# The second MLP's up projection as seven block products per pair of column tiles

## The chip, the cores and the metric

The kernel runs on one core of one Trainium2 chip. A core has five engines that run their own queues and meet at semaphores: TensorE (PE in the profile, its weight loads PEld), VectorE (DVE), ScalarE (ACT), GpSimd (POOL) and SyncE (SP), which here issues the loads. The metric is the device time of one execution in microseconds (us), lower is better. The median of three runs stands for a kernel.

## What is computed

Two transformer blocks for 1024 tokens of width 1024, all in fp32. The change lies in the last part of the second block:

```
h2 = rmsnorm(x, mlp_norm_g)
x = x + square(relu(h2 @ w_ff1)) @ w_ff2      # w_ff1 1024x4096, w_ff2 4096x1024
return rmsnorm(x, final_norm_g)
```

The kernel doesn't divide by the root mean square before the MLP. Since relu and square are homogeneous it carries x times the gains through both products, and takes the mean square of each token in as a factor on the residual (MS2) and in the last norm.

## The kernel before

Activations lie transposed: features on the 128 partitions, 1024 tokens along the free dimension, 8 chunks of 1024 columns for the width. PSUM has 8 banks of 512 fp32 columns. Every fp32 operand of a product is written as a high part (rounded to the matmul's type, fp32r) and a low part (the rest), and a product is three matmuls: high by high, high by low, low by high. A matmul takes a 128x128 tile of weights and 512 tokens.

The second MLP works through the 4096 hidden features in 8 groups of 512 (`mlp_products`, `mlp_act`, `mlp_dve`, `mlp_loads`, `mlp_splits`). A group has 8 weight tiles. Four are up tiles: 128 hidden columns, 8 chunks of contraction, 3 products and 2 token halves, which is 48 matmuls (L1213) into two banks. Four are down tiles: 256 output columns, 4 chunks of contraction, again 48 matmuls (L1223), into four banks. Banks 0 to 3 and 4 to 7 take turns. For each weight tile SP loads 512 KB into one of two RAW buffers, GpSimd writes the high part WHI (L782) and the low part WLO (L784), and TensorE waits for `s_w`. After an up tile ScalarE takes the relu from PSUM (L1731) and squares it into F2H (L1733), VectorE squares it in fp32 (L2405) and subtracts (L2408, F2L). After a down tile VectorE adds four banks to the sum F2SUM (L2421). The first additions are preceded by the residual times MS2 (L2416).

Ahead of the MLP stand 8 output products of the attention (`product`, L930), 48 matmuls each. After each of them VectorE adds it to X (L2660), ScalarE squares and makes the high part A2H, VectorE the low part A2L (L2664) and the sum of squares. Within the first group TensorE also makes the sums of squares per token (`root_sums`) and spreads their roots over the partitions (`root_spread`). The last group's down products (`last_down`, L1502) go in 8 pieces of 24 matmuls by token halves, with the transposes of finished token blocks (`final_t`) among them; ScalarE (`final_root`) and VectorE (`final_out`, L2691) close each block, and SP stores it.

The first MLP has, at its head and tail, blocks of half the tokens: 24 matmuls into one bank (`half_up`, L1160). Their relu and square go by halves of 512 tokens: ScalarE L1716 and L1718, VectorE `hidden_squared` (L2287, one input from PSUM) and `hidden_low` (L2295, both inputs from SBUF), and ScalarE makes the weights' high part, GpSimd the low part.

## Time and profile before

| what | value |
| --- | --- |
| median of three runs | 2884.7 us (2882.3, 2884.7, 2892.6) |
| span of the profiled execution | 2887.8 us |
| time of the profiled execution beside its span | the page gives the span alone |
| TensorE busy | 2805.4 us, 97% of the span, 14772 matmuls |
| mean granted TensorE clock | 0.991 of 2.4 GHz |
| VectorE, ScalarE, GpSimd busy | 51%, 26%, 36% |

Times in rows count from the start of the span. "x192" is a number of instructions. In the chain of work that ended last each row is a start, a length in us and the work that filled it; "issue" is time in which nothing shown was waited for. PEclk is the granted clock of TensorE, 1.00 at full speed.

### The profile page before, as it was taken

What the parts mean: (1) busy time and instruction counts of PE and PEld (TensorE: products, weight loads), DVE (VectorE), ACT (ScalarE), POOL (GpSimd) and SP (SyncE); (2) the same over time, 40 slices, a digit from 0 to 9 for tenths busy, and PEclk for the clock granted to TensorE, in tenths of its full rate; (3) what the DMA queues carried; (4) which work ended last, traced back from release to release, by engine and by line L of the source; (5) the groups of instructions that cost most, each with busy time, mean ns of one, the idle gap of its engine ahead of it and who ended that gap; (6) DMA issues with size and microseconds to landing.
All of it is one profiled execution on the core that took longest, in us unless ns stands there. A gap on an engine that the chain in (4) does not pass through costs nothing.

```text
span 2887.8 us, 36086 instructions
## 1 busy us (share of the span) xinstructions
PE 2805.4 (97%) x14772; PEld 2249.2 (78%) x14772; DVE 1467.7 (51%) x1829; ACT 741.4 (26%) x1092; POOL 1039.1 (36%) x462
## 2 busy tenths in 40 slices
PE   7999999999999999999999999899999999999998
PEld 4888887778888887776888466577888888888887
DVE  4853244643333334556999534996555423333324
ACT  5001124432011013454121456753111100011101
POOL 1433324444444444442132032101344444444434
PEclk9999999999999999999999999999999999999999
DMA  8531114222111122253132100002411111111112
GB/s 309 187 112 37 37 43 140 88 88 87 52 51 44 51 66 88 88 161 69 44 106 95 37 1 2 2 2 100 149 51 44 45 51 51 44 50 51 44 58 102
DMA packets 256236, 211.34 MB, mean 73 GB/s; under 512 B 23131, under 2 KB 240746, under 8 KB 255722
## 3 DMA queue, kind: packets, MB, share of 16 engines
q1 hardware_dynamic: 253082, 201.12, 22.7%
q10 hardware_dynamic: 3024, 8.39, 0.8%
q8 instruction: 93, 1.52, 0.2%
q14 instruction: 37, 0.30, 0.0%
HBM read 187.46 MB, written 20.97 MB: 72 GB/s over the span
## 4 chain that ended last, share of the span: by engine, by line
PE 80%; DVE 14%; ACT 3%; issue 2%; POOL 1%; DMA 0%; SPq 0%; ACTq 0%; DVEq 0%; POOLq 0%
PE PS L1213 18%; PE PS L1223 17%; PE PS L930 13%; PE PS L1160 9%; DVE MB L2490 6%; PE PS L1176 5%; PE PS L1460 3%; PE PS L914 3%; PE PS L1367 2%; PE PS L1425 2%; PE PS L1502 1%; DVE STEP L2592 1%; PE PS L1398 1%; DVE NMX L2624 1%; PE PS L1278 1%
## 5 line engine op out<-in xcount | busy, mean ns | idle before, releaser
L782 POOL TENSOR_TENSOR WHI<-RAW,ZERO 128x1024 fp32r<-128x1024 f32 x148 | 283.5, 1916 | 1079.1 <-PE PS L1213 284.9
L795 POOL TENSOR_TENSOR WLO<-RAW,WHI 128x1024 fp32r<-128x1024 f32 x112 | 269.8, 2410 | 475.4 <-ACT WHI L1617 475.4
L784 POOL TENSOR_TENSOR WLO<-RAW,WHI 128x1024 fp32r<-128x1024 f32 x148 | 407.0, 2750 | 11.6
L930 PE MATMUL PS<-H,WHI 128*128 128x512 f32 x864 | 271.0, 395 | 2.5 <-DVE L L2639 0.9
L1731 ACT ACTIVATE RL<-PS 128x1024 f32<-128x1024 f32 x48 | 49.3, 1027 | 870.8 <-PE PS L1213 870.8
L930 PE MATMUL PS<-L,WHI 128*128 128x512 f32 x864 | 267.4, 391 | 0.0
L930 PE MATMUL PS<-H,WLO 128*128 128x512 f32 x864 | 267.0, 390 | 0.0
L2405 DVE TENSOR_TENSOR FT<-RL 128x1024 f32<-128x1024 f32 x48 | 92.8, 1934 | 316.9 <-ACT RL L1731 316.9
L1617 ACT ACTIVATE WHI<-RAW 128x1024 fp32r<-128x1024 f32 x112 | 118.7, 1060 | 468.8 <-PE PS L1160 188.3
L1160 PE MATMUL PS<-H,WHI 128*128 128x512 f32 x496 | 197.5, 398 | 5.0 <-POOL WLO L795 4.4
L1160 PE MATMUL PS<-L,WHI 128*128 128x512 f32 x496 | 194.7, 392 | 0.0
L1160 PE MATMUL PS<-H,WLO 128*128 128x512 f32 x496 | 194.7, 392 | 0.0
L930 PEld LDWEIGHTS PS<-L,WHI 128*128 128x128 f32 x864 | 162.8, 188 | 34.6
L930 PEld LDWEIGHTS PS<-H,WHI 128*128 128x128 f32 x864 | 160.4, 189 | 37.7 <-issue 2.4
L930 PEld LDWEIGHTS PS<-H,WLO 128*128 128x128 f32 x864 | 162.7, 188 | 34.5
L2490 DVE TENSOR_SCALAR_CACHE_REDUCE MB<-SCO,CAND 128x384 bf16<-128x384 f32 (+2 forms) x198 | 174.3, 943 | 1.2
L2421 DVE TENSOR_TENSOR F2SUM<-F2SUM,PS 128x2048 f32<-128x2048 f32 x28 | 64.1, 2288 | 200.2 <-PE PS L1223 200.2
L1213 PE MATMUL PS<-A2H,WHI 128*128 128x512 f32 x512 | 157.8, 389 | 1.4 <-issue 1.4
L1213 PE MATMUL PS<-A2H,WLO 128*128 128x512 f32 x512 | 157.6, 389 | 0.0
L1213 PE MATMUL PS<-A2L,WHI 128*128 128x512 f32 x512 | 157.6, 389 | 0.0
L2624 DVE TENSOR_REDUCE NMX<-PS 128x1 f32<-128x128 f32 (+26 forms) x128 | 92.7, 724 | 124.5 <-PE PS L1370 110.1
L1223 PE MATMUL PS<-F2H,WHI 128*128 128x512 f32 x448 | 138.0, 389 | 1.3 <-ACT MS L1958 1.3
(384 smaller groups left out, 5498.9 us busy)
## 6 DMA issues: line engine op xcount, KB each, us to landing
RAW<-w_fc SPq DMA_DIRECT2D x96, 512.0 KB, 3.9
RAW<-w_ff SPq DMA_DIRECT2D x68, 512.0 KB, 3.6
RAW<-w_in SPq DMA_DIRECT2D x62, 512.0 KB, 4.0
ADA<-w_ada SPq DMA_DIRECT2D x32, 512.0 KB, 5.1
RAW<-w_out SPq DMA_DIRECT2D x24, 512.0 KB, 4.0
ADA_FIRST<-w_ada SPq DMA_DIRECT2D x16, 512.0 KB, 10.2
X<-x_scratch SPq DMA_DIRECT2D x2, 4096.0 KB, 13.6
GB<-gate_scratch SPq DMA_DIRECT2D x8, 1024.0 KB, 5.5
```

Of the source, the lines that this page charges most:

```text
L782: nc.gpsimd.tensor_add(WHI[j][:, 0:n], RAW[j][:, 0:n], ZERO[:, 0:1].to_broadcast([P, n])).then_inc(s_whi, 1)
L784: nc.gpsimd.tensor_sub(WLO[j][:, 0:n], RAW[j][:, 0:n], WHI[j][:, 0:n].bitcast(F32)).then_inc(s_w, 1)
L795: nc.gpsimd.tensor_sub(WLO[w % 2][:, :], RAW[w % 2][:, :], WHI[w % 2][:, :].bitcast(F32)).then_inc(s_w, 1)
L930: last = mm(bank(b + t), wt[:, k, :], half(a, (k + at) % KC, t), start=(k == 0 and n == 0), stop=(k == KC - 1 and n == 2))
L1160: last = mm(bank(w_bank(w)), wt[:, k, :], half(a, k, e), start=(k == 0 and n == 0), stop=(k == KC - 1 and n == 2))
L1176: last = mm(bank(w_bank(w) + c), wt[:, k, c * P:(c + 1) * P], half(a, k, e), start=(k == 0 and n == 0), stop=(k == 3 and n == 2))
L1213: last = mm(bank(b + t), wt[:, k, :], a[:, k * S + t * HALF:k * S + (t + 1) * HALF], start=(k == 0 and n == 0), stop=(k == KC - 1 and n == 2))
L1223: last = mm(bank(b + 2 * c + t), wt[:, k, c * P:(c + 1) * P], a[:, k * S + t * HALF:k * S + (t + 1) * HALF], start=(k == 0 and n == 0), st ...
L1617: A(WHI[w % 2][:, :], RAW[w % 2][:, :], ACT.Copy).then_inc(s_whi, 1)
L2405: V.tensor_tensor(FT[:, :], RL[i % 2][:, :], RL[i % 2][:, :], ALU.mult).then_inc(s_h32, 1)
L2490: V.tensor_scalar(mask(b), scores(b), CAND[:, b - 2:b - 1].bitcast(F32), 0.0, op, ALU.add, accum_out=REACH[:, b - 2:b - 1]).then_inc(s_dve, 1)
L2624: V.reduce_max(NMX[:, n % 2:n % 2 + 1], bank(2 * (n % 2), 2)[:, 0:w], AX, negate=True).then_inc(s_nm, 1)
```

## The change

The up projection of the second MLP is done by Strassen's identity in Winograd's form. The 4096 hidden columns are taken in 16 pairs of 128-column tiles (`PAIR_GROUPS2`). For a pair the product is a 2x2 block product: hidden tile (2), contraction half (2, four chunks each), token half (2, 512 tokens). Instead of eight block products it makes seven, `pair_unit(g, j)`, each of 12 matmuls (4 chunks, 3 products, 512 tokens) into one bank.

- The seven token-side operands (blocks AH and AL 0 to 6, each 4 pieces of 512) are sums and differences of the four quarters of the scaled x. VectorE and ScalarE make them while the output products run; block 5 and block 6 are made in the first pair.
- The weight-side operands: four of the seven are sums, made in place by VectorE (`weight_sum`, 128x512, four for each pair). ScalarE writes the high part of each (`unit_high`), GpSimd the low part (`unit_low`), through a ring of four buffers of 512 (QHI, QLO). A high part waits until the unit four before it has been multiplied.
- The results are combined by quadrants (hidden tile, token half). ScalarE copies the first product (P1C), VectorE adds it to the second and fifth (`second_read`, `third_read`), adds those to three quadrants (`quadrant_added`); for each of four quadrants ScalarE takes relu and square (high part), VectorE the fp32 square in PSUM (`quadrant_squared`) and the low part (`quadrant_low`).
- The down projection has the same number of matmuls, but now per pair: 4 tiles (256 output columns, 2 chunks) of 24 matmuls into four banks (`pair_down`), so VectorE's additions of four banks to the sum are 14 times 4 in place of 7 times 4. The first down tile of a pair takes the quadrants in turn, 6 matmuls each, and waits for each one's low part. F2SUM is now X itself.
- Loads: two of 512 KB for the two up tiles of a pair, when the seventh low part of the pair before is done, and four of 256 KB through two buffers DRAW; the third waits for the low part of the pair's first down tile.
- The last two pairs have their up products back to back, then come the 8 last down pieces, each as two units of 12 matmuls. ScalarE makes the high parts of all sixteen before `final_root`.
- All of it is written out instead of looped.

The core of the diff (regions, the loads, the loops of each engine; what prepares blocks 0 to 6, the final additions and `load_last` are left out):

```diff
-        A2H = region("A2H", K0, 8 * S, F32R)
-        A2L = region("A2L", Y0, 8 * S, F32R)
-        F2H = region("F2H", L0, 4 * S, F32R)
-        F2L = region("F2L", L0 + 4096, 4 * S, F32R)
-        F2SUM = region("F2SUM", H0, 8 * S)
-        MS2 = region("MS2", K0 + 12288, S)
-        GAIN = region("GAIN", X0, S)
-        OT = [region(f"OT{j}", K0 + 1024 * j, S) for j in range(4)]
+        BLOCK_AT = [K0, K0 + 8192, K0 + 4096, K0 + 12288, K0 + 16384, L0, L0 + 4096]
+        AH = [region(f"AH{j}", a, 4 * HALF, F32R) for j, a in enumerate(BLOCK_AT)]
+        AL = [region(f"AL{j}", a + 2048, 4 * HALF, F32R) for j, a in enumerate(BLOCK_AT)]
+        ACC2 = region("ACC2", K0 + 20480, S)
+        MS2 = region("MS2", K0 + 20480, S)
+        QRAW = [region(f"QRAW{j}", 1024 * j, S) for j in range(2)]
+        QHI = [region(f"QHI{j}", 2048 + HALF * j, HALF, F32R) for j in range(4)]
+        QLO = [region(f"QLO{j}", 4096 + HALF * j, HALF, F32R) for j in range(4)]
+        F2H = [region(f"F2H{j}", a, 2 * S, F32R) for j, a in enumerate([H0, K0])]
+        F2L = [region(f"F2L{j}", a + 2048, 2 * S, F32R) for j, a in enumerate([H0, K0])]
+        P1C, U2, U3 = [region(n, H0 + 4096 + HALF * j, HALF) for j, n in enumerate(["P1C", "U2", "U3"])]
+        RLQ = [region(f"RLQ{j}", H0 + 5632 + HALF * j, HALF) for j in range(2)]
+        DRAW = [region(f"DRAW{j}", H0 + 6656 + HALF * j, HALF) for j in range(2)]
+        F2SUM = X
...
+        UNIT_SOURCE = ((0, 0), (0, 0), (1, 0), (0, 1), (1, 0), (1, 1), (0, 1))
+        SUMMED = {2: 1, 1: 2, 4: 3, 6: 4}
+        QUADRANTS = [(0, 0), (1, 1), (1, 0), (0, 1)]
+        QUADRANT_BANK = [0, 1, 3, 2]
...
+            def load_up(g):
+                for j in range(2):
+                    if g:
+                        sp.wait_ge(s_w, MLP2 + unit(g - 1, 6) + 1)
+                    else:
+                        sp.wait_ge(s_w, MLP2 - 1 + j)
+                    sp.dma_start(k_n(QRAW[j], KC, P), w_tile(w_ff1_2, 0, KC, 256 * g + P * j, P)).then_inc(s_raw[j], 16)
+            def load_down(g, c):
+                n = 4 * g + c
+                if n >= 2:
+                    sp.wait_ge(s_w, MLP2 + unit((n - 2) // 4, 7 + (n - 2) % 4) + 1)
+                else:
+                    sp.wait_ge(s_mm, MLP2)
+                sp.dma_start(k_n(DRAW[c % 2], 2, 256), w_tile(w_ff2_2, 256 * g, 2, 256 * c, 256)).then_inc(q_draw[c % 2], 16)
...
+            load_up(0)
+            load_down(0, 0)
+            load_down(0, 1)
+            for g in range(PAIR_GROUPS2 - 2):
+                load_up(g + 1)
+                load_down(g, 2)
+                load_down(g, 3)
+                if g + 1 < PAIR_GROUPS2 - 2:
+                    load_down(g + 1, 0)
+                    load_down(g + 1, 1)
+            load_last(0)
+            load_last(1)
+            load_up(PAIR_GROUPS2 - 1)
+            for i in range(2, 6):
+                load_last(i)
...
+            def unit_low(n, src):
+                pool.wait_ge(s_whi, MLP2 + n + 1)
+                nc.gpsimd.tensor_sub(QLO[n % 4][:, :], src, QHI[n % 4][:, :].bitcast(F32)).then_inc(s_w, 1)
...
+                for j in range(7):
+                    tile, at = UNIT_SOURCE[j]
+                    if j in SUMMED:
+                        pool.wait_ge(q_sum, 4 * g + SUMMED[j])
+                    unit_low(n + j, piece(QRAW[tile], at))
+                if g < PAIR_GROUPS2 - 2:
+                    for c in range(4):
+                        unit_low(n + 7 + c, DRAW[c % 2][:, :])
...
+            def pair_unit(g, j):
+                n = unit(g, j)
+                b = step_bank(pair_step(g)) + {0: 0, 3: 0, 1: 1, 4: 1, 2: 2, 6: 2, 5: 3}[j]
+                pe.wait_ge(s_w, MLP2 + n + 1)
+                if j == 0 and g == 0:
+                    pe.wait_ge(*reads(OUT0 + 6))
+                if j == 0 and 1 <= g < PAIR_GROUPS2 - 1:
+                    pe.wait_ge(s_evv, M2.dve + 4 * g - 1)
+                if j == 0 and g == PAIR_GROUPS2 - 1:
+                    pe.wait_ge(s_evv, M2.dve + 4 * (g - 1))
+                if j == 2 and g == 0:
+                    pe.wait_ge(*added(2 * KC - 1))
+                if j == 3:
+                    pe.wait_ge(q_sq, act_read(g, "p1"))
+                if j == 4:
+                    pe.wait_ge(q_read, dve_read(g, "u2"))
+                if j == 6:
+                    pe.wait_ge(q_read, dve_read(g, "c1"))
+                second = j in (3, 4, 6)
+                hi, lo = k_n(QHI[n % 4], 4, P), k_n(QLO[n % 4], 4, P)
+                for k in range(4):
+                    if g == 0:
+                        pe.wait_ge(e_lo, COMBO_AT[j, k])
+                    for p, (wt, a) in enumerate(((hi, AH[j]), (hi, AL[j]), (lo, AH[j]))):
+                        last = mm(bank(b), wt[:, k, :], piece(a, k), start=(not second and k == 0 and p == 0),
+                                  stop=(k == 3 and p == 2), skip_group_check=True)
+                last.then_inc(s_mm, 1)
...
+            def pair_down(g, c):
+                n = unit(g, 7 + c)
+                b = step_bank(pair_step(g) + 1 + c)
+                pe.wait_ge(s_w, MLP2 + n + 1)
+                if c == 0 and g == 0:
+                    pe.wait_ge(s_ms2, 1)
+                if c == 0 and g:
+                    pe.wait_ge(s_evv, M2.dve + 4 * g)
+                if c == 1:
+                    pe.wait_ge(q_read, dve_read(g, "fl3"))
+                if c >= 2:
+                    pe.wait_ge(s_evv, M2.dve + 4 * g + c - 1)
+                hi, lo = k_n(QHI[n % 4], 2, 256), k_n(QLO[n % 4], 2, 256)
+                for q, (k, e) in enumerate(QUADRANTS):
+                    if c == 0:
+                        pe.wait_ge(q_read, dve_read(g, f"fl{q}"))
+                    for cc in range(2):
+                        for p, (wt, a) in enumerate(((hi, F2H[0]), (hi, F2L[0]), (lo, F2H[0]))):
+                            last = mm(bank(b + 2 * cc + e), wt[:, k, cc * P:(cc + 1) * P], quarter(a, k, e),
+                                      start=(q < 2 and p == 0), stop=(q >= 2 and p == 2))
+                last.then_inc(s_mm, 1)
...
+            for g in range(PAIR_GROUPS2):
+                for j in range(7):
+                    pair_unit(g, j)
+                    if g == 0 and j == 2:
+                        root_sums()
+                    if g == 0 and j == 4:
+                        root_spread()
+                if g < PAIR_GROUPS2 - 2:
+                    for c in range(4):
+                        pair_down(g, c)
...
+            def unit_high(n, src):
+                if n == 0:
+                    act.wait_ge(s_w, MLP2)
+                if n < 4:
+                    act.wait_ge(s_mm, MLP2 - 1 + n // 2)
+                else:
+                    act.wait_ge(s_mm, MLP2 + n - 3)
+                A(QHI[n % 4][:, :], src, ACT.Copy).then_inc(s_whi, 1)
...
+            for j in range(4):
+                up_high(0, j)
+            for g in range(PAIR_GROUPS2):
+                first_copied(g)
+                high_after(g, 4)
+                if g == 0:
+                    for k in range(2):
+                        act.wait_ge(e_t, SUM_AT[5, k])
+                        sum_high(5, k, bank(4 + k))
+                high_after(g, 5)
+                if g == 0:
+                    for k in range(2, 4):
+                        act.wait_ge(e_t, SUM_AT[5, k])
+                        sum_high(5, k, bank(2 + k))
+                    for k in range(4):
+                        sum_high(6, k, half(X, 4 + k, 1), gain(4 + k))
+                high_after(g, 6)
+                if g == 0:
+                    root(7, 6)
+                quadrant_relu(g, 0)
+                quadrant_high(g, 0)
+                if g != PAIR_GROUPS2 - 2:
+                    high_after(g, 7)
+                    high_after(g, 8)
+                quadrant_relu(g, 1)
+                quadrant_high(g, 1)
+                if g == 0:
+                    act.wait_ge(s_bc, 7)
+                    A(MS2[:, :], bank(6, 2), ACT.Square).then_inc(s_ms2, 1)
+                if g != PAIR_GROUPS2 - 2:
+                    high_after(g, 9)
+                quadrant_relu(g, 2)
+                quadrant_high(g, 2)
+                high_after(g, 10 if g != PAIR_GROUPS2 - 2 else 7)
+                quadrant_relu(g, 3)
+                quadrant_high(g, 3)
+                if g == PAIR_GROUPS2 - 2:
+                    for j in (8, 9, 10):
+                        high_after(g, j)
+                if g < PAIR_GROUPS2 - 2:
+                    for j in range(4):
+                        high_after(g, UNITS + j)
+            for i in range(4, 16):
+                last_high(i)
...
+            def weight_sum(g, m):
+                if m == 1:
+                    dve.wait_ge(s_raw[1], up_in(1, g))
+                    V.tensor_add(x21, x21, x22).then_inc(q_sum, 1)
+                if m == 2:
+                    dve.wait_ge(q_sum, 4 * g + 1)
+                    dve.wait_ge(s_w, MLP2 + unit(g, 0) + 1)
+                    V.tensor_sub(x11, x21, x11).then_inc(q_sum, 1)
+                if m == 3:
+                    dve.wait_ge(q_sum, 4 * g + 2)
+                    dve.wait_ge(s_w, MLP2 + unit(g, 2) + 1)
+                    V.tensor_sub(x21, x22, x11).then_inc(q_sum, 1)
+                if m == 4:
+                    dve.wait_ge(s_w, MLP2 + unit(g, 3) + 1)
+                    V.tensor_sub(x12, x12, x11).then_inc(q_sum, 1)
+            def pair_read(g, before_last=None):
+                second_read(g)
+                quadrant_squared(g, 0)
+                quadrant_low(g, 0)
+                third_read(g)
+                quadrant_added(g, 1)
+                quadrant_squared(g, 1)
+                quadrant_added(g, 2)
+                quadrant_low(g, 1)
+                quadrant_squared(g, 2)
+                quadrant_low(g, 2)
+                if before_last is not None:
+                    before_last()
+                quadrant_added(g, 3)
+                quadrant_squared(g, 3)
+                quadrant_low(g, 3)
...
+            for g in range(1, PAIR_GROUPS2 - 2):
+                pair_read(g)
+                for c in range(4):
+                    down_added(g, c)
+                    if g + 1 < PAIR_GROUPS2 - 1:
+                        weight_sum(g + 1, c + 1)
+            pair_read(PAIR_GROUPS2 - 2, lambda: weight_sum(PAIR_GROUPS2 - 1, 1))
+            for m in range(2, 5):
+                weight_sum(PAIR_GROUPS2 - 1, m)
+            pair_read(PAIR_GROUPS2 - 1)
```

## Rows read from the trace of the kernel before

**Rows 1.** The page: busy time by engine, and granted clock in 40 slices of the span.

```profile
PE 2805.4 (97%) x14772; PEld 2249.2 (78%) x14772; DVE 1467.7 (51%) x1829; ACT 741.4 (26%) x1092; POOL 1039.1 (36%) x462
...
PEclk9999999999999999999999999999999999999999
```

**Rows 2.** Chain of work that ended last, whole span: the MLP's groups.

```profile
2259.68 43.52 PE PS L1213 x192
...
2781.92 43.53 PE PS L1213 x192
```

**Rows 3.** The same chain around the start of the second MLP.

```profile
2165.76 1.36 issue
2167.12 22.03 PE PS L1213 x96
...
2214.81 1.01 ACT MS L1958
...
2215.87 43.81 PE PS L1223 x192
```

**Rows 4.** The same chain in the last 100 us.

```profile
2828.60 3.28 DVE F2L L2408
...
2831.93 23.46 PE PS L1502 x102
...
2857.14 5.49 PE PS L1502 x24
...
2864.38 10.90 PE PS L1502 x48
...
2877.50 1.12 ACT RL L1966 x2
...
2879.17 1.17 DVE OT L2691
```

**Rows 5.** The same chain in a half block of the first MLP.

```profile
1053.33 21.77 PE PS L1160 x96
```

**Rows 6.** Groups of VectorE, 1100 to 1260 us: busy, mean ns of one | idle before.

```profile
L2295 DVE TENSOR_TENSOR FL<-RL,FH 128x512 fp32r<-128x512 f32 x12 | 15.8, 1313 | 0.3
...
L2218 DVE SCALAR_TENSOR_TENSOR X<-PS,MODA,X 128x512 f32<-128x512 f32 x12 | 9.0, 749 | 0.3
L2287 DVE SCALAR_TENSOR_TENSOR RL<-PS,RL 128x512 f32<-128x512 f32 x12 | 8.3, 691 | 31.8 <-ACT RL L1716 31.8
```

**Rows 7.** Timeline of a half block: start, length in us.

```profile
1076.18 0.58 ACT L1716 ACTIVATE RL<-PS 128x512 f32<-128x512 f32 x1
1076.35 2.39 POOL L795 TENSOR_TENSOR WLO<-RAW,WHI 128x1024 fp32r<-128x1024 f32 x1 [3.04 <-ACT WHI L1617]
1076.79 0.63 ACT L1718 ACTIVATE FH<-RL 128x512 fp32r<-128x512 f32 x1
...
1077.52 1.77 DVE L2295 TENSOR_TENSOR FL<-RL,FH 128x512 fp32r<-128x512 f32 x1
```

**Rows 8.** GpSimd's subtraction of 512 columns: shortest, median, longest in ns.

```profile
L805 POOL TENSOR_TENSOR L<-N32A,H x8: 1286/1293/1742, 514.5 to 1284.7; 128x512 fp32r<-128x512 f32 x8
```

**Rows 9.** Timeline at the boundary of two down tiles in the loop.

```profile
2400.96 0.61 PE L1223 MATMUL PS<-F2H,WHI 128*128 128x512 f32 x2
2401.16 2.29 DVE L2421 TENSOR_TENSOR F2SUM<-F2SUM,PS 128x2048 f32<-128x2048 f32 x1 [4.46 <-PE PS L1223]
```

**Rows 10.** Groups of VectorE, 2150 us to the end.

```profile
L2416 DVE TENSOR_TENSOR F2SUM<-X,MS 128x2048 f32<-128x2048 f32 x4 | 15.3, 3816 | 0.0
```

**Rows 11.** Loads: KB each, median us from issue to landing.

```profile
RAW<-w_ff SPq DMA_DIRECT2D x68, 512.0 KB, 3.6
...
RAW<-w_in SPq DMA_DIRECT2D x3, 256.0 KB, 3.2
```

**Rows 12.** Two windows: busy of PE, PEld, DVE, ACT, POOL, then granted clock, DMA share, GB/s.

```profile
434.00:438.00 4.00, 2.03 (x9) 1.33 (x8) 0.00 (x0) 3.08 (x5) 1.94 (x1) 1.00 1.00 434
438.00:442.00 4.00, 3.54 (x9) 2.83 (x10) 0.00 (x0) 1.06 (x2) 2.74 (x2) 0.57 1.15 483
```

More of the change, by code:

```diff
@@ L767, in _ @@
+            sp.wait_ge(s_mm, MLP2 + unit(PAIR_GROUPS2 - 1, 1) + 1)
+            n = VCOL["final_norm_g_2"]
+            sp.dma_start(GAIN[:, :], vec[n:n + KC, :].rearrange("k p -> (k p)").partition_broadcast(P)).then_inc(s_gain, 16)
+            for i in range(6, 16):
+                load_last(i)
             for t in range(NB):
@@ L1184, in _, with mlp_products, group @@
                 half_up(W_OUT0 + h, h // 8, (H, L), None, 0 if h >= 8 else None, h - 8)
[L1186 removed]
+            def mlp_products(m, acts, hidden):
                 (act_hi, act_lo), (hid_hi, hid_lo) = acts, hidden
[L1189 to L1194 removed]
+                def group(g):
+                    for i in range(8):
                         w = 8 * g + (m.w + i)
@@ L1226, in group @@
                         last.then_inc(s_mm, 1)
[L1227 to L1237 removed]
+                with pe.Fori(HEAD, GROUPS - TAIL) as g:
+                    group(g)
             def half_blocks(m, blocks, q):
@@ L1733, in group @@
                         A(chunk(hid_hi, i), RL[i % 2][:, :], ACT.Square).then_inc(s_hi, 1)
-                        if first and between is not None and i in between:
-                            between[i]()
-                if start == 0:
-                    group(0, True)
-                    with act.Fori(1, GROUPS) as g:
-                        group(g, False)
-                else:
-                    with act.Fori(HEAD, GROUPS - TAIL) as g:
-                        group(g, False)
+                with act.Fori(HEAD, GROUPS - TAIL) as g:
+                    group(g)
             act.wait_ge(s_lo, M1.lo + 8 * HEAD)
-            mlp_act(M1B, FH, start=HEAD)
+            mlp_act(M1B, FH)
             def tail_act(n, i):
```

444 lines of the change are left out of this document (313 added, 131 removed).

## The prediction

> **What bounds the kernel now.** I read the page first: TensorE is busy 97% of the span, VectorE about half, at a clock that is full in every slice [rows 1]. Then the chain of work that ended last. Through the second MLP it is TensorE alone, in 13 pieces of 192 matmuls without a gap between them [rows 2]: 43.52 / 192 = 0.2267 us a matmul. So here a removed matmul is worth its full time, as long as nothing else becomes late. Then the two ends. At the start 1.36 us pass after the last output product, and from its end (2165.76) to the end of the first group (2215.87 + 43.81 = 2259.68) 93.92 us go by for 384 matmuls, worth 87.04: 6.9 us are lost there [rows 3]. At the tail the chain goes through VectorE's F2L before the last down products [rows 4]; the up products end at 2781.92 + 43.53 = 2825.45, 18 matmuls can still be done until 2829.53, and the next begins at 2831.93: 2.4 us lost.
>
> **What the change removes.** Seven products of 12 matmuls in place of 96 for each pair: 12 fewer, in 16 pairs 192 fewer, 192 x 0.2267 = **43.5 us**. The down products stay at 1536. A unit of 12 (2.72 us) is shorter than any tile in this loop; 24 into one bank, each tile with its own waits, run at 21.77 / 96 = 0.2268 [rows 5], so I take the same pace.
>
> **What the steady pairs cost.** A pair is 180 matmuls, 40.80 us: units 0 to 6 until 19.04 (t = 0 at the pair's first matmul), then four down tiles of 5.44. Load is no issue: VectorE has 13 quadrant steps, 4 additions and 4 weight sums, 13 x 0.7 + 4 x 2.29 + 4 x 1.2 = 23 us of 40.8; ScalarE 20 operations of about 0.6; GpSimd 11 x 1.3. The latency is. Prices: a VectorE step of 512 with one input in PSUM 0.69 or 0.75 [rows 6]; with both in SBUF between that (nearest row without GpSimd's price, 0.69) and 1.77, what it took while GpSimd subtracted [rows 6, 7]: mean 1.31, I take 1.2. Relu 0.58 and square 0.63 on ScalarE [rows 7]; I take 0.63 for a high part too. GpSimd 1.29 [rows 8]. From the end of a product to its reader about 0.2 [rows 9], from one engine to another 0.03 [rows 7]. All quadrant steps have a PSUM operand, so I give them 0.69.
>
> The schedule: unit 3 ends at 10.9. ScalarE: relu and square of quadrant 0 until 12.4, high part of the first down tile until 13.0. GpSimd's low part: 14.3. Only that lets SP issue the third down load. 512 KB land in 3.6, 256 KB in 3.2 [rows 11]; I take 3.3, bounds 3.0 and 4.2. It lands at 17.7, its high part is done at 18.35, and this stands in ScalarE's queue ahead of the relu of quadrant 2, otherwise ready at 17.3. Relu 18.9, VectorE's square 19.6, low part 20.4, and only then comes the addition for quadrant 3 (21.1), though unit 6 ended at 19.04. Relu 21.7, square 22.4, low part 23.15. TensorE reaches quadrant 3 after 18 matmuls of the first down tile, 19.04 + 4.08 = 23.12. So the chain just misses. A restart after a wait costs 22.03 - 21.76 = 0.27 [rows 3]. I take 0.28 a pair, with 13 pairs (1 to 13) **3.6 us**; the lower end is 0 (landing at 3.0), the upper 0.9 more a pair (landing at 4.2, or each step 0.1 longer). VectorE's additions (2.29) stay ahead of the banks' next use by 3 us each, and the two up loads have 15 us.
>
> **The opening.** After the last output product come, in order on ScalarE: VectorE's add of 1024 (1.3), three high parts of block pieces (2.1, with a short wait), the square of 1024 (1.0) and only then the first high part of a weight (0.63), GpSimd 1.3. TensorE starts at 6.6 where it now waits 1.36. Unit 1 needs the second weight sum, queued on VectorE behind two low parts and the last square's addition: 1.7 more. The roots are asked for after unit 4, but ScalarE first makes blocks 5 and 6 (six high parts) and waits for their sums: 3.4. The sums and spreads themselves, now also there, take 1.7 + 1.9. Quadrant 3 misses by 0.4, restarts 0.8. Together 16.5 of waits and extras until the first pair is done, against the 6.9 now: **+9.6 us**. Bounds: 12 SBUF steps of VectorE at 0.7 or at 1.77 instead of 1.2 move it by -3 or, with the residual's multiplications at up to twice 2.29 (mean 3.8 [rows 10]) that delay the second pair, by +9.
>
> **Pair 14 to 15.** No down tiles lie between. ScalarE's queue has the first high part of pair 15 behind quadrant 2's square: GpSimd is done 1.5 after unit 6 ends. The second weight sum waits for it and for quadrant 3's steps on VectorE, and unit 1 for that sum's high and low part: 3.1 more. With two restarts **+5.1 us**.
>
> **Last quadrant.** The first 12 last-down matmuls need only pair 14, and cover 2.72 of about 3.1. A loss of 0.4 and a restart in place of 2.4: **-2.0 us** (within 1 either way).
>
> **The end.** Now the transposes of blocks 2 and 3 follow piece 5 directly [rows 4]; they need `final_out(0)`. After the change ScalarE makes all sixteen high parts first, and the sixteenth waits for the end of piece 5. Only then `final_root(0)`: 0.3 + 0.6, then square, root, reciprocal and output, which take 2880.34 - 2877.50 = 2.84 [rows 4] and a little: 4.0, then 0.5 for block 3 and restarts: **+4.9 us**. Nothing catches this up, as pieces 6 and 7 stand behind it on TensorE.
>
> **The clock.** TensorE had 2.03 us of work in 434 to 438, and in the 4 us after it the granted clock was 0.57, a mean of the full 2.4 and the half 1.2 GHz: 4 x 0.43 = 1.7 lost, then full again [rows 12]. The opening wait of 6.6 is emptier, the one at the end similar: **+2.0**, bounds 0 and 4. The Trainium skill (TensorE: Matmul & The Clock Gate, "Part 1: The HAM clock gate") says that the array's clock falls to half after an idle stretch and comes back only under sustained work. The two windows agree with it; by the page the term stands, and without it the sum below would be -22.3.
>
> **Sum:** -43.5 + 9.6 + 3.6 + 5.1 - 2.0 + 4.9 + 2.0 = -20.3 us. The differences come from one execution whose span is 2887.8; the median 2884.7 is 0.1% from it, so I set the difference against the median: **2864 us**.
>
> **Rivals.**
> - *The pairs slip.* The third down load or a step is late as in the upper bound: 0.9 x 14 = 12.6 more, **2877**. For it: no slack in the schedule at all. Against: 256 KB rows at 3.2. Chance 0.17.
> - *Shorter waits.* Landing at 3.0, no port conflicts in the opening, no clock loss: -3.6 - 4 - 2, **2854**. For it: GpSimd is idle much of the opening, and successive VectorE steps overlap a little. Chance 0.22.
> - *The other side: VectorE's quadrant chain is slower than a PSUM step.* Ten steps lie between unit 4's end and the last low part, in a window of 9.5 us. At 1.0 us each (between 0.69 and the 1.77 of L2295) every pair waits 3.1 more, 43 us: **2907**, slower. It decides from (20.3 + 14.4) / 14 = 2.5 us a pair, 0.94 a step. For it: L2295, the same low part, took 1.31 on average. Against: its inputs were both in SBUF, and steps with a PSUM input stood at 0.69 to 0.75 while GpSimd was half busy. Chance 0.06. [...]
> - *The change doesn't save what it says.* If each of the 184 units and down tiles paid 0.15 us at its boundary, 28 us would go: **2892**. Against: the pace in [rows 5]. Chance 0.05.
>
> **How the numbers follow.** The forecast has 0.5, with 2859 to 2871 of its own. 0.5% is 14.4 us, about what a measurement can tell from no change: faster is below 2870.3. That takes the shorter waits and nearly all of the forecast, 0.22 + 0.46 = 0.68; slower is the VectorE chain, 0.06; the rest, 0.26, lies between. The range leaves out the ends of the two near rivals and the far ones: 2852 to 2878.
>
> **What the changed profile would show.** TensorE with 192 fewer matmuls of 512 and the same 0.2267 inside a unit. A wait of about 6.6 us before the first unit, ended by GpSimd; one of 1.7 and one of 3.4 in the first pair. Pairs 1 to 13 starting 41.1 us apart: 40.8 would mean that the chain fits, 42 or more that it slips. Third down load issued 14.3 after the pair's start, landing at 17.7. Quadrant steps at 0.69; over 0.9 the forecast is wrong. Waits of 1.5 and 3.1 at pair 15, and 4 at the transposes of block 2. The prediction fails if the loads land much later, or if an engine's queue order holds up a step that I took as ready.

## The result and the profile after

The changed kernel takes **2862.0 us** (median of 4 executions, 2860.9 to 2868.8) against 2885.7 for the kernel before (4, 2882.3 to 2892.6). The ratio is 0.9916 with a 95% interval of 0.9898 to 0.9933, so 24 us faster (19 to 29), where 2864 was forecast. The profiled execution took 2860.9 us, 1.8 more than its span of 2859.1.

The page of the changed kernel, which answers to [rows 1]:

```profile
PE 2767.5 (97%) x14580; PEld 2215.1 (77%) x14580; DVE 1563.1 (55%) x2109; ACT 882.8 (31%) x1380; POOL 953.6 (33%) x510
```

TensorE has exactly the 192 matmuls fewer. To see what became of their 43.5 us I measured both traces between the same two events, which the change leaves in place: the end of the last output product, and the end of the last output that VectorE writes. This **stretch** is 2884.62 - 2165.76 = 718.9 us before (the last output ends at 2884.62) and 2855.90 - 2164.61 = 691.3 after: 27.6 gained.

The chain of work that ended last, as [rows 2] and [rows 3] have it for before. Columns: start, length, work.

```profile
2100.00 64.61 PE PS L1041 x285
...
2201.34 18.02 PE PS L1631 x78
2219.36 19.04 PE PS L1608 x84
```

The last output product ends at 2164.61 and the first pair at 2219.36, 54.75 later. Its 180 matmuls are worth 40.80, so 13.95 are lost, where 6.9 were before. The waits of TensorE in that stretch (in total, times, longest):

```profile
PE PS L1608 <- POOL QLO L1001: 6.4, 1, 6.4
PE PS L1579 <- ACT SS L1705: 1.1, 1, 1.1
PE PS L1631 <- DVE F2L L3028: 0.4, 1, 0.4
```

Three windows behind the output product (busy PE and its matmuls, granted clock, DMA share, GB/s) and four matmuls of the timeline:

```profile
2164.60:2171.00 6.40, 0.04 (x1) 0.73 0.25 82
2171.00:2175.00 4.00, 4.00 (x11) 0.58 0.00 0
2175.00:2179.00 4.00, 4.00 (x19) 1.00 0.02 4
```

```profile
2170.96 0.80 PE L1608 MATMUL PS<-AH,QHI 128*128 128x512 f32 x1 [6.36 <-POOL QLO L1001]
...
2173.26 0.63 PE L1608 MATMUL PS<-AH,QLO 128*128 128x512 f32 x1
2173.69 0.63 PE L1608 MATMUL PS<-AH,QHI 128*128 128x512 f32 x1
...
2175.37 0.40 PE L1608 MATMUL PS<-AH,QHI 128*128 128x512 f32 x1
```

From the second to the eighth the matmuls start 0.42 to 0.43 us apart instead of 0.2267, which is the lower of the clock's two levels. The first eight take 3.49 us until the ninth starts, 1.7 more than at full speed. Unit 1 begins with the matmul at 2175.37, without a wait of its own.

The steady pairs, in the same chain:

```profile
2238.40 21.84 PE PS L1631 x96
2260.24 19.04 PE PS L1608 x84
2279.28 21.76 PE PS L1631 x96
...
2728.19 21.76 PE PS L1631 x96
2749.95 13.61 PE PS L1608 x60
```

From 2219.36 to 2749.95 are 530.6 us for 13 pairs, 40.81 each. 180 x 0.2267 is 40.80, and TensorE's list of waits is empty for this part. Eleven of the 13 take 40.80; the 0.2 us beyond are in pair 1 (21.84 for its down tiles instead of 21.76) and pair 8 (21.87). VectorE and ScalarE inside pair 1, which began at 2219.36, show how near the others were; the last line is the last F2L of pair 3, which began at 2301.04:

```profile
2236.92 0.63 ACT L2133 ACTIVATE QHI<-DRAW 128x512 fp32r<-128x512 f32 x1 [1.21 <-DMA DRAW<-w_ff]
2237.46 0.58 ACT L2174 ACTIVATE RLQ<-PS 128x512 f32<-128x512 f32 x1
```

```profile
2238.80 0.69 DVE L3028 TENSOR_TENSOR F2L<-PS,F2H 128x512 fp32r<-128x512 f32 x1
2239.41 0.69 DVE L3014 TENSOR_TENSOR PS<-PS,U 128x512 f32<-128x512 f32 x1
...
2241.50 0.69 DVE L3028 TENSOR_TENSOR F2L<-PS,F2H 128x512 fp32r<-128x512 f32 x1
...
2322.63 0.69 DVE L3028 TENSOR_TENSOR F2L<-PS,F2H 128x512 fp32r<-128x512 f32 x1
```

ScalarE does wait for the third down load, until 17.56 into the pair, and the relu that it needs more stands behind it in its queue. The last F2L ends at 22.83 into the pair, while TensorE would reach it at 19.04 + 4.08 = 23.12 if nothing held it up. Pair 1 is one of the two latest: in pair 3 the last F2L ends at 22.28, in pair 8 at 22.90, and in the other ten at 22.15 to 22.45. Pairs 1 and 8 are the two that ran longer, so the limit lies some 0.3 below 23.12. Steps and loads, by groups of 2219 to 2750 and by the page's list of DMA issues (KB each, us to landing):

```profile
L3020 DVE SCALAR_TENSOR_TENSOR PS<-PS,RLQ 128x512 f32<-128x512 f32 x52 | 36.4, 700 | 95.2 <-ACT RLQ L2174 95.2
...
L3045 DVE TENSOR_TENSOR QRAW<-QRAW,QRAW 128x512 f32<-128x512 f32 x13 | 9.0, 694 | 0.0
```

```profile
DRAW<-w_ff SPq DMA_DIRECT2D x62, 256.0 KB, 2.7
```

The last 110 us, which answer to [rows 4]:

```profile
2774.95 1.28 POOL QLO L1001
...
2776.28 16.67 PE PS L1608 x72
...
2795.90 24.77 PE PS L1662 x108
2820.67 1.75 PE PS L1025 x16
2822.42 5.50 PE PS L1662 x24
...
2831.58 1.29 DVE OT L3100
...
2832.92 1.85 PE PS L1025 x8
2834.77 11.79 PE PS L1662 x48
...
2854.62 1.28 DVE OT L3100
```

Pairs 14 and 15 take 45.95 us for 40.80 of work; TensorE waits 1.3 and 2.9 for GpSimd's low parts, the second time until 2776.28. From 2795.90 to the last output's end are 60.00 us. Before it was 52.69 from 2831.93, with six matmuls (1.36) fewer in that run. The wait is in the transposes (L1025): half of them run, then 3.6 pass until an output leaves.

### The profile page after: what moved, and what is told of

Read it like the earlier page. It is cut to its first block, busy times and chain, and to the rows that moved or that the text cites. A ratio compares the mean times of both kernels' runs of the same rounds, so it can differ in the third digit from the quotient of the medians.

```text
span 2859.1 us, 36276 instructions
## 1 busy us (share of the span) xinstructions
PE 2767.5 (97%) x14580; PEld 2215.1 (77%) x14580; DVE 1563.1 (55%) x2109; ACT 882.8 (31%) x1380; POOL 953.6 (33%) x510
## 3 DMA queue, kind: packets, MB, share of 16 engines
q8 instruction: 107, 1.75, 0.3%
## 4 chain that ended last, share of the span: by engine, by line
PE 78%; DVE 15%; ACT 3%; issue 2%; POOL 1%; DMA 0%; SPq 0%; ACTq 0%; DVEq 0%; POOLq 0%
PE PS L1041 14%; PE PS L1631 11%; PE PS L1608 10%; PE PS L1271 10%; DVE MB L2757 6%; PE PS L1318 6%; PE PS L1328 6%; PE PS L1287 5%; PE PS L1557 3%; PE PS L1025 3%; PE PS L1464 2%; PE PS L1522 2%; PE PS L1662 1%; DVE STEP L2859 1%; PE PS L1495 1%
## 5 line engine op out<-in xcount | busy, mean ns | idle before, releaser
L888 POOL TENSOR_TENSOR WLO<-RAW,WHI 128x1024 fp32r<-128x1024 f32 x112 | 269.8, 2409 | 475.0 <-ACT WHI L1772 475.0
L875 POOL TENSOR_TENSOR WHI<-RAW,ZERO 128x1024 fp32r<-128x1024 f32 x80 | 154.6, 1932 | 692.9 <-PE PS L1041 235.8
L1001 POOL TENSOR_TENSOR QLO<-QRAW,QHI 128x512 fp32r<-128x512 f32 x122 | 158.9, 1305 | 356.1 <-ACT QHI L2133 356.0
L877 POOL TENSOR_TENSOR WLO<-RAW,WHI 128x1024 fp32r<-128x1024 f32 x80 | 211.7, 2646 | 6.3
L3074 DVE TENSOR_TENSOR X<-X,PS 128x2048 f32<-128x2048 f32 x56 | 128.1, 2288 | 127.4 <-PE PS L1631 127.3
L1608 PE MATMUL PS<-AH,QHI 128*128 128x512 f32 x448 | 175.7, 392 | 10.6 <-POOL QLO L1001 10.6
L2133 ACT ACTIVATE QHI<-QRAW 128x512 fp32r<-128x512 f32 x122 | 76.4, 630 | 325.7 <-PE PS L1631 135.3
L1608 PE MATMUL PS<-AL,QHI 128*128 128x512 f32 x448 | 175.0, 391 | 0.0
L1631 PE MATMUL PS<-F2H,QHI 128*128 128x512 f32 x448 | 174.6, 390 | 0.4 <-DVE F2L L3028 0.4
L1608 PE MATMUL PS<-AH,QLO 128*128 128x512 f32 x448 | 174.8, 390 | 0.0
L1631 PE MATMUL PS<-F2L,QHI 128*128 128x512 f32 x448 | 174.3, 389 | 0.0
```

What stands on the lines that cost most here:

```text
L875: nc.gpsimd.tensor_add(WHI[j][:, 0:n], RAW[j][:, 0:n], ZERO[:, 0:1].to_broadcast([P, n])).then_inc(s_whi, 1)
L877: nc.gpsimd.tensor_sub(WLO[j][:, 0:n], RAW[j][:, 0:n], WHI[j][:, 0:n].bitcast(F32)).then_inc(s_w, 1)
L888: nc.gpsimd.tensor_sub(WLO[w % 2][:, :], RAW[w % 2][:, :], WHI[w % 2][:, :].bitcast(F32)).then_inc(s_w, 1)
L1001: nc.gpsimd.tensor_sub(QLO[n % 4][:, :], src, QHI[n % 4][:, :].bitcast(F32)).then_inc(s_w, 1)
L1608: last = mm(bank(b), wt[:, k, :], piece(a, k), start=(not second and k == 0 and p == 0), stop=(k == 3 and p == 2), skip_group_check=True)
L1631: last = mm(bank(b + 2 * cc + e), wt[:, k, cc * P:(cc + 1) * P], quarter(a, k, e), start=(q < 2 and p == 0), stop=(q >= 2 and p == 2))
```

## Experiments

The stretch in the profiled execution is the sharper measure, since nothing from ahead of the MLP is in it. The kernel before was run again, and so was the changed one. Each ratio in the table is taken against executions of the kernel before on the same chip (medians 2889.5, 2886.6 and 2888.2 us for the three later sets), so medians of different sets don't compare directly.

> The kernel before, unchanged, for a second trace beside the first. Its second MLP, from the end of the last output product to the last VectorE output, took 718.9 us in the first trace, and what lies ahead of it 2165.8. The changed kernel's trace has 691.3 and 2164.6, so the second MLP gained 27.6 us there, while the medians differ by 23.7. If the change acts in the second MLP alone and always by the same amount, this trace has 718.9 again within 0.5 us, and the missing 4 us lie ahead of it as plain variation from execution to execution. If the second MLP itself varies, this stretch differs by some us.

> The changed kernel again, unchanged. The traces so far show that what lies ahead of the second MLP ends between 2158 and 2166 us from one execution to the next, in code that no kernel here changes. Measured from the end of the last output product to the last VectorE output, the second MLP should take 691.3 us again, within 1 us or so (where the clock falls after a wait can move it), against 718.9 and 720.5 in the two traces of the kernel before.

| kernel | median, us | ratio to before, 95% interval | stretch, us |
| --- | --- | --- | --- |
| before, first trace | 2885.7 | | 718.9 |
| before again | 2888.4 (before on that chip 2889.5) | 0.9996 (0.9984 to 1.0008) | 720.5 |
| changed, first trace | 2862.0 | 0.9916 (0.9898 to 0.9933) | 691.3 |
| changed again | 2864.1 | 0.9915 (0.9893 to 0.9938) | 691.5 |
| third down load later | 2871.5 | 0.9937 (0.9917 to 0.9956) | 706.2 |
| the same, relu ahead of its high part | 2860.9 | 0.9890 (0.9874 to 0.9907) | 691.9 |
| one quadrant step more | 2863.8 | 0.9903 (0.9886 to 0.9919) | 698.1 |
| first roots of the end earlier | 2856.3 | 0.9887 (0.9864 to 0.9910) | 686.9 |
| pair 15's parts earlier | 2856.9 (2855.1 without the outlier named below) | 0.9891 (0.9864 to 0.9918) | 685.9 |
| opening's parts earlier | 2859.1 | 0.9893 (0.9875 to 0.9912) | 691.5 |
| end and pair 15 | 2851.1 | 0.9875 (0.9858 to 0.9893) | 680.4 |
| end, pair 15 and opening | 2847.6 | 0.9859 (0.9842 to 0.9876) | 677.5 |

The stretch repeats within 0.2 for the changed kernel. The 1.6 between the two traces of before lie in the run of 102 last down matmuls, 25.07 against 23.46 [rows 4], with a granted clock of 0.61 in the window 2828 to 2832. What stands ahead of the stretch, the same code but for a few instructions in one kernel or another, ended between 2158.0 and 2166.7 after the start. That scatter is as large as what single experiments change, so their verdicts below rest on the stretch of one execution each. The medians don't resolve all of them: by its ratio the kernel with one quadrant step more isn't slower than the changed one.

**The third down load a wait later.** SP issues it, and what is behind it, only after the pair's second down tile has its low part. In pair 1 it is issued 15.72 us after the pair's start instead of 14.09, 1.6 later:

```diff
-                    sp.wait_ge(s_w, MLP2 + unit((n - 2) // 4, 7 + (n - 2) % 4) + 1)
+                    sp.wait_ge(s_w, MLP2 + unit((n - 2) // 4, 7 + (n - 2) % 4) + 1 + (c == 2))
```

> The third down load of each pair waits for the low part of the second down tile instead of the first, so it is issued some 1.6 us later. Everything else as in the changed kernel. Theory (the quadrant chain is on the edge: in the changed kernel's second pair the last low part ends 22.8 us after the pair's start, TensorE wants it at 23.1; the third load's high part stands ahead of the relu of quadrant 2 in ScalarE's queue): the chain is later by 1.6, TensorE waits 1.3 to 1.6 in each of 14 pairs with a restart of 0.1 to 0.3, 20 to 25 us more, about 2884. Rival (loads have room, since the third down tile is multiplied only 29.9 us after the pair's start): no change, 2862.

The stretch grew by 14.9, below the theory's bracket but far from the rival's nothing. TensorE's waits and ScalarE around the load:

```profile
PE PS L1631 <- DVE F2L L3028: 10.4, 13, 1.0
```

```profile
2232.17 0.63 ACT L2133 ACTIVATE QHI<-DRAW 128x512 fp32r<-128x512 f32 x1 [2.73 <-DMA DRAW<-w_ff]
2232.71 0.58 ACT L2174 ACTIVATE RLQ<-PS 128x512 f32<-128x512 f32 x1
```

A wait of 0.8 on average in each of 13 pairs, where none had been listed. Pair 1 began at 2213.08, so the high part starts at 19.09 instead of 17.56, 1.53 later. Over the 13 pairs the last F2L ends at 23.91 into the pair on average instead of 22.38, also 1.53 later. The pairs come (2758.47 - 2213.08) / 13 = 41.95 apart, 1.15 more than 40.80, of which 0.8 is the listed wait and 0.35 the restart behind it. So some 0.4 of the 1.53 were free on average. The chain from the load to the last low part is the predicted one; what it lacked was to be late.

**The same delay, with the relu and high part of quadrant 2 ahead of the third down tile's high part** in ScalarE's queue:

```diff
-                if g != PAIR_GROUPS2 - 2:
-                    high_after(g, 9)
                 quadrant_relu(g, 2)
                 quadrant_high(g, 2)
+                if g != PAIR_GROUPS2 - 2:
+                    high_after(g, 9)
```

> The same late load, but ScalarE's high part of the third down tile is queued behind the relu and square of quadrant 2 instead of ahead of them. Theory (it is the queue order that lets a load hold up the quadrants): the loss of the run with the late load is gone, 2862, pairs 40.8 us apart. Rival (the late load costs through GpSimd or through its own tile): still 20 us slower.

```profile
2234.70 21.76 PE PS L1631 x96
2256.45 19.04 PE PS L1608 x84
```

All but 0.6 of the 14.9 us is back (691.9), with the same late load: the 13 pairs take 530.4 us, 40.80 each, without a wait. What is left lies elsewhere: behind the wait at pair 15, 72 matmuls took 18.24 us instead of 16.67. It was the order of ScalarE's queue that made the load count for TensorE, not the data.

**One more step of 512 on VectorE** ahead of quadrant 2's low part, into an unused buffer:

```diff
                 quadrant_squared(g, 2)
+                extra_low(g, 2)
                 quadrant_low(g, 2)
```

> One more VectorE subtraction of 512 columns from PSUM (written to a buffer nobody reads) and a wait for it, ahead of quadrant 2's low part in pairs 1 to 15: 0.72 us more in the quadrant chain. Theory (slack of 0.3 us): pairs 1 to 13 each wait 0.4 and pay 0.1 to 0.3 for the restart, 7 to 9 us in all, about 2870. Rival (VectorE is busy just 55% and the step is hidden): no change, 2862.

The stretch is 6.8 us longer, but not all of it in the pairs that the theory spoke of. Pairs 1 to 13 take 535.15 us (2213.93 to 2749.08), 4.7 more than 13 x 40.80, 0.36 a pair for a step that puts the last F2L 0.75 later (23.13 into the pair on average). Another 2.3 came in pairs 14 and 15 (48.2 instead of 45.95), where the wait before the last quadrant is 1.0 and 48 matmuls behind the wait of 2.9 took 12.80 us, where the full pace gives 10.88, at a granted clock of 0.76 and 0.82 in the windows 2774 to 2778 and 2778 to 2782. A chain with no slack would have paid 0.75 a pair, 9.8 us; one with ample slack nothing. So again some 0.4 us were free on average. Pair by pair the runs with the extra step, with the late load and without either agree: a pair is longer than 40.80 by as much as its last F2L ends after about 22.8.

**The end: the first two roots ahead of the last two high parts.**

```diff
-            for i in range(4, 16):
-                last_high(i)
...
+            for i in range(4, 14):
+                last_high(i)
             act.wait_ge(s_mm, MLP2 + LAST_UNIT)
-            for t in range(NB):
+            for t in range(2):
+                final_root(t, FINAL_BANKS[t])
+            for i in range(14, 16):
+                last_high(i)
+            for t in range(2, NB):
                 final_root(t, FINAL_BANKS[t])
```

> The changed kernel with one thing moved: ScalarE computes the roots of token blocks 0 and 1 behind the fourteenth of the last sixteen high parts, no longer behind the sixteenth. Theory (TensorE's 3.6 us wait at the transposes of block 2 comes from ScalarE's queue order): that wait and the fall of the clock behind it go, the second MLP's stretch is 5 us shorter, 686. Rival (the wait moves to the high parts of the last units, which now stand behind the roots, or to the outputs): gain below 2 us.

```profile
2825.37 5.49 PE PS L1662 x24
2830.86 1.75 PE PS L1025 x16
2832.61 10.90 PE PS L1662 x48
```

The wait is gone and so is the slow run behind it, 10.90 for 48 matmuls where there had been 11.79. From the start of the 108 matmuls to the last output it is 54.0 us instead of 60.0, and these make up nearly all of it: the 3.6, a second wait of 0.3, the 0.9, and 1.0 by which the eight transposes behind the wait had been slower (1.85 us, where sixteen take 1.75 at full speed). The stretch fell by 4.6 only, since 1.3 were lost elsewhere (72 matmuls of pair 15 in 17.94 instead of 16.67, with a granted clock of 0.65 in the window 2778 to 2782).

**Pair 15: on ScalarE its first high part ahead of quadrant 2 and the next three ahead of quadrant 3, on VectorE its first two weight sums (for its second and third unit) ahead of quadrant 2's square.**

```diff
+                if g == PAIR_GROUPS2 - 2:
+                    high_after(g, 7)
                 quadrant_relu(g, 2)
                 quadrant_high(g, 2)
-                high_after(g, 10 if g != PAIR_GROUPS2 - 2 else 7)
+                for j in (10,) if g != PAIR_GROUPS2 - 2 else (8, 9, 10):
+                    high_after(g, j)
...
                 quadrant_squared(g, 1)
+                if early is not None:
+                    early(1)
                 quadrant_added(g, 2)
                 quadrant_low(g, 1)
+                if early is not None:
+                    early(2)
                 quadrant_squared(g, 2)
                 quadrant_low(g, 2)
-                if before_last is not None:
-                    before_last()
...
-            pair_read(PAIR_GROUPS2 - 2, lambda: weight_sum(PAIR_GROUPS2 - 1, 1))
-            for m in range(2, 5):
+            pair_read(PAIR_GROUPS2 - 2, lambda m: weight_sum(PAIR_GROUPS2 - 1, m))
+            for m in range(3, 5):
```

> The changed kernel with the preparation of the last pair moved forward: in pair 14 ScalarE makes the first high part of pair 15 ahead of the relu of quadrant 2, and the next three ahead of that of quadrant 3; VectorE makes the first two weight sums between the quadrant steps of pair 14, whose results nobody needs soon. Theory (the two waits of 1.3 and 2.9 us at pair 15 are queue order): both go, the stretch is 4 to 5 us shorter, 687. Rival (pair 15's up loads land too late for it, since they are issued when the low part of pair 14's last unit is done): one wait of 1 to 3 us stays, gain 1 to 3.

```profile
2745.88 38.09 PE PS L1608 x168
2786.94 24.77 PE PS L1662 x108
```

The 168 matmuls of both pairs run through, and 5.5 us are gained, 4.9 of them here. (One of the four timed executions took 11025 us, which no other of any kernel did, and I have no cause. The median of all four is 2856.9; without it it is 2855.1, and the ratio in the table leaves it out.)

**The opening: the first two high parts and weight sums of the MLP ahead of the last steps of the norm, and the roots on ScalarE ahead of block 5's last two pieces and block 6.**

```diff
                     A(bank(6), half(X, k, 1), ACT.Copy, scale=gain(k)).then_inc(e_hi, 1)
+                    if i == 7:
+                        up_high(0, 0)
+                        up_high(0, 1)
...
                 if g == 0:
+                    root(7, 6)
                     for k in range(2, 4):
                         act.wait_ge(e_t, SUM_AT[5, k])
...
                 high_after(g, 6)
-                if g == 0:
-                    root(7, 6)
...
                     block_value(bank(7), 2, k)
+                    if i == 7:
+                        weight_sum(0, 1)
+                        weight_sum(0, 2)
```

> The changed kernel with the opening reordered: ScalarE makes the first two high parts of weights and VectorE the first two weight sums while the last output product still runs, and ScalarE takes the roots before blocks 5 and 6. Theory (the whole opening is a chain through the queues of VectorE and ScalarE): unit 0 starts at once, unit 1 waits some 2 us for block 1, the clock stays up, and the first pair ends about 50 instead of 54.8 us after the last output product: 5 us shorter, stretch 686. Rival (VectorE's own work, blocks 4 to 6, sets the end of the first pair, and the 6.4 us wait only moves to later units): gain below 2.

The stretch stayed at 691.5, which is the rival's number. But the trace shows that the opening did gain: the first pair ends 51.5 after the last output product (2214.43 - 2162.92), 3.3 sooner. Of TensorE's 6.4 us wait two remained, of 0.8 and 3.3, so it moved in part, as the rival has it; the granted clock stayed at 1.00 in the three windows from 2163 to 2175, and the wait for the roots is gone. The 13 steady pairs took 530.4. Of the 3.3, 2.9 went at pair 15 and the rest at the end (60.7 instead of 60.0):

```profile
2744.83 13.61 PE PS L1608 x60
...
2771.16 19.56 PE PS L1608 x72
```

```profile
2770.00:2774.00 4.00, 2.84 (x7) 0.57 0.01 4
2774.00:2778.00 4.00, 4.00 (x12) 0.58 0.00 0
```

The same 72 matmuls behind the same wait of 2.9 took 2.9 us longer, at a granted clock of 0.57 and 0.58, where both windows of the changed kernel's trace have 1.00. The move of the opening isn't needed for that: the same matmuls took 18.24 with the reordered late load and 17.94 with the end's move, and 16.63 in two other traces. The traced execution was also the slowest of its five, whose median of 2859.1 us (2854.6 to 2859.4) lies 5 below that of the changed kernel on the same chip (2860.2 to 2866.6). If the fall of the clock ate the gain, it must come out in a kernel that no longer has the wait. Two kernels were made for that, one with the moves at the end and at pair 15, one with the opening's too.

> Both moves at once: the first roots of the end before the last two high parts, and pair 15's early high part and second and third weight sum ahead of pair 14's. The stretch from the last output product's end to the last output was 691.3 to 691.5 us in two executions of the changed kernel, 686.9 with the end's move alone (in which the first of pair 15's matmuls ran for 1.3 us longer at a lower clock than without it) and 685.9 with pair 15's move alone. Theory (two separate waits in one chain of TensorE's work, with the clock's fall behind each): they add up, 691.4 less 4.6 less 5.5 is 681.3, less up to 1.3 more because there is no wait left behind which the clock can fall at pair 15; so 680 to 681.5, a time near 2852. Rival (one move gives back what the other gains): 685 or more, a time near 2857.

> The same with the opening's move added: the first weight sums and high parts of the MLP ahead of the last of the norm's. By itself that brought the first pair's end to 51.5 us after the last output product where it had been 54.8, and yet the stretch stayed at 691.5: the 72 matmuls behind pair 15's second wait took 19.56 us where they had taken 16.67, with a granted clock of 0.57 and 0.58 in the two 4 us windows behind that wait where there had been 1.00. Theory (the gain is real and was eaten by a fall of the clock behind a wait that this kernel no longer has): 3.3 us below the kernel with two moves, a stretch of 677 to 678.5 and a time near 2849. Rival (the matmuls between the opening and pair 15 never keep what the opening gains): the same stretch as with two moves, 680 to 681.5.

```profile
2748.20 38.09 PE PS L1608 x168
2789.25 24.75 PE PS L1662 x108
2814.01 1.75 PE PS L1025 x16
2815.75 5.49 PE PS L1662 x24
2821.24 1.75 PE PS L1025 x16
2822.99 10.90 PE PS L1662 x48
```

680.4 with two moves and 677.5 with three, both inside what the theories of adding gains gave: the gains add up, and the opening's 2.9 is kept where no wait follows that the clock can fall behind. With all three, 2847.6 us is 1.4% below the kernel before and some 15 us below the changed one (0.9859 / 0.9915 = 0.9944). Its stretch is 42 us below the mean of the two of before (719.7), nearly what 192 matmuls are worth. Not every loss is gone: the opening takes 52.1 us for 40.80 of work, so 11.3 are lost there where it was 6.9 before. Against that stand the wait before the last down products, 0.3 instead of 2.4, and the slower last pieces in the second trace of before.

## Why the prediction was right, point by point

The time was forecast within 2 us, but that is better than the working deserves. Each step against the stretch, where the measured numbers split one stretch of 691.3 against one of 718.9:

| step | predicted | measured | from |
| --- | --- | --- | --- |
| 192 matmuls fewer | -43.5 | -43.5 | 40.80 for 180 matmuls in the steady pairs |
| opening | +9.6 | +5.3 | 13.95 - 6.9 = 7.05, of it 1.7 by the clock |
| steady pairs | +3.6 | +0.2 | 530.6 - 13 x 40.80 |
| pairs 14, 15 and last quadrant | +5.1 - 2.0 = +3.1 | +2.75 | 5.15 lost, 2.4 before |
| end | +4.9 | +5.05 | 60.00 - 52.69 - 1.36 = 5.95, of it 0.9 by the clock |
| clock | +2.0 | +2.6 | 4 x 0.42 in the opening, 11.79 - 10.90 at the end |
| sum | -20.3 | -27.6 | |

**The clock** fell where it was expected, in the opening and at the end. The Trainium skill (TensorE: Matmul & The Clock Gate, "Part 1: The HAM clock gate") agrees in its direction: idle lowers it, sustained work restores it.

**Two terms were too large.** The steady pairs were costed with the third load issued at 14.3 and landing at 17.7, 3.3 later with some rounding up. It was issued at 14.09, and its high part started at 17.56 in pair 1, 17.62 in pair 8 and 16.9 to 17.2 in the other eleven, so the landing was nearer to the lower bound of 3.0 (the page's 2.7 is a median over all loads of 256 KB). The last low part came at 22.38 on average and not at 23.15. Since the term was made of restarts (0.28 each), this error of 0.8 took nearly all of it. The lower bound of 0 had been kept for just this case. But the prediction also had TensorE's need too late, 23.12 where the runs show some 22.8: its own 23.15 would have cost 0.4 a pair, 5 us. The late load and the extra step show that the margin is thin, some 0.4 on average, and the reordering that it hangs on ScalarE's queue.

**The opening** lost 4.3 less than predicted. The first wait was right (6.4 against 6.6), and so were the sums (1.84 against 1.7) and spreads (2.05 against 1.9). The wait before unit 1, 1.7 in the prediction, wasn't there: GpSimd had its low part done at 2174.28, 9.7 after the last output product instead of the predicted 6.6 + 2.72 + 1.7 = 11.0, and unit 0 ran at the lower clock and ended only at 2175.4. At full speed it would have ended at 2173.7, and some 0.6 of the wait would have shown, an estimate from these times. So the two losses overlap, and I had counted both. The wait for the roots was 1.1, not 3.4. ScalarE did wait for block 5's last two sums (L2977), 2.7 and 0.8, but it was through with blocks 5 and 6 at 2187.2, ahead of unit 4's end at 2188.1. Ahead of the roots stood only one more high part and a table load, which the prediction doesn't name:

```profile
2187.75 1.28 ACT L1705 ACT_TABLE_LOAD   x1
```

Which of the six high parts it had too late can't be said, since it gives no times for them. The bound of +9 by slow multiplications of the residual didn't show either: the first of them took 2.28.

**Pair 15 and the last quadrant** were right by place and size: waits of 1.3 and 2.9 by GpSimd's low parts against 1.5 and 3.1, and 0.3 before the last quadrant against 0.4. (The sum's -2.0 leaves out the restart that the text beside it names; with its 0.3 the term would be -1.7.) **The end** too: 3.6 at the transposes of block 2 against 4.0. Moving the named instructions removed the two waits at pair 15 and the one at the end, each in its own experiment; the 0.3 before the last quadrant stayed in all of them.

**Price of a weight sum.** I took 1.2 for two inputs in SBUF. In the steady pairs they cost 0.68 to 0.69; in pair 1 GpSimd is idle at each of the four. Beside a busy GpSimd the same instruction took 1.69, near the 1.77 of [rows 7]. The quadrant steps, with a PSUM operand, stayed at 0.69 to 0.70, the one at 2239.41 too, while GpSimd subtracted from 2239.30 on, and with that the rival of the slow VectorE chain falls. The 2907 and 2892 us of the far rivals left no trace: no quadrant step was slow, and with pairs of 40.80 no boundary cost anything.

```profile
2171.49 0.69 DVE L3041 TENSOR_TENSOR QRAW<-QRAW,QRAW 128x512 f32<-128x512 f32 x1
...
2176.13 1.69 DVE L3045 TENSOR_TENSOR QRAW<-QRAW,QRAW 128x512 f32<-128x512 f32 x1 [0.46 <-POOL QLO L1001]
```

GpSimd was busy from 2173.03 to 2177.27, not at 2171.49.

**And yet the median agreed.** By the parts the time should have fallen by 27.6, by the medians it fell by 23.7. The trace on which the sum was made had a span of 2887.8; with the 1.8 that lie around a span it was an execution of about 2889.6, 5 above the median of that set, while the profiled execution of the changed kernel was 1.2 below its own. Setting the difference against the median without that correction made the forecast 5 us too low, and two terms that were too large by 7.7 made it too high. The two errors nearly cancel, by luck, and the number was 2 us off. What makes one execution differ from another by 5 us and more ahead of the MLP, in code that both kernels share, wasn't looked into and stays open.

## What to carry to other kernels

Here one engine was 97% busy and the chain of waits was that engine alone, and fewer instructions on it paid in full inside the loop. The question moved to the seams: the 192 matmuls were worth 43.5 us, the steady loop gave back 0.2 and three seams 16. Of these 16, 14 could be had back by moving a few instructions up in the queues of ScalarE and VectorE: nearly all at pair 15 and at the end, which were lost to queue order, and only 2.9 of some 7 in the opening, whose rest wasn't tested. Before you trust a schedule that "just fits", find the instruction that stands in a queue ahead of what the critical engine needs and waits for something else: a load late by 1.5 us in each of 13 pairs cost 15 us in all while such an instruction stood ahead, and nothing in the pairs once it stood behind.

## What the runs showed of the hardware

- The same wait can cost differently. Behind TensorE's wait of 2.9 us at pair 15, 72 matmuls took 16.67 and 16.63 us in two traces of the changed kernel, 16.63 with the late load, and 17.94, 18.24 and 19.56 in three other kernels; the windows behind the wait show a granted clock of 1.00 in the first and of 0.65, 0.57 and 0.57 in the last three. In the kernel before, 102 matmuls behind a wait of 2.4 us took 23.46 us in one trace and 25.07 in the other. So it varies between executions of one kernel. A gain ahead of such a wait can vanish in it, and taking the wait away can be worth more than its length.
- With two inputs in SBUF a VectorE operation of 128x512 took 0.69 us with GpSimd idle and 1.69 and 1.78 with it busy beside them. The quadrant steps, with one input in PSUM, took 0.69 to 0.70.
- The last output product ended between 2158.0 and 2166.7 us after the start in twelve traces, with nearly the same code ahead of it. Comparing stretches between two fixed events, rather than spans, repeated within 0.2 us for the changed kernel and 1.6 for the kernel before, and a single trace can be off by up to 3 us where a wait is left that the clock may fall behind.
